# Feed-forward up-projections with the tokens' high and low parts in one 512-column matmul, on one Trainium2 core

## The chip, the cores and the metric

The kernel runs on one core of one Trainium2 chip. The metric is the device time of one launch in microseconds (us); lower is better. The engines of a core are named as in the profile: PE (matrix multiply), PEld (its weight loads), DVE (vector), ACT (scalar), POOL (GpSimd) and SP (which issues the DMAs here).

## What is computed

Two small decoder blocks are run one after the other over the same 256 tokens of width 1024, batch 1, all in float32. The first block has two layers (a gated linear attention layer and a sparse attention layer, each with attention over a memory), and each layer ends in a convolutional feed-forward. The second block has one layer, with a plain gated feed-forward. These three feed-forwards, with an inner width of 2816, are what the change touches:

```python
def conv_ffn(h, w_up, conv_w, conv_b, w_down):
    T = h.shape[1]
    a, b = jnp.split(h @ w_up, 2, axis=-1)
    a_pad = jnp.pad(a, ((0, 0), (CONV_WIDTH - 1, 0), (0, 0)))
    a = sum(a_pad[:, j:j + T] * conv_w[j] for j in range(CONV_WIDTH)) + conv_b
    return (jax.nn.silu(a) * b) @ w_down
...
    n2 = _rmsnorm(h, norm2_w)
    ffn = (jax.nn.silu(n2 @ w_gate.astype(h.dtype)) * (n2 @ w_up.astype(h.dtype))) @ w_down.astype(h.dtype)
    return h + ffn
```

## The kernel before, in words

**Tiling.** Activations lie transposed: 128 partitions are 128 of the 1024 features, and the columns are the 256 tokens (8 chunks c of 128 features). Every float32 matrix product of the projections is made of three matmuls in the type fp32r, a type with fewer bits than float32. Each operand is split into a high part (rounded to fp32r) and a low part (the rest): weights into `wh` and `wl`, tokens into `xh` and `xl`. `mm3` (lines 359 to 362) adds high weights times high tokens, high weights times low tokens, and low weights times high tokens into the same 256 columns of a PSUM bank. The RMS norm's factor per token (`rs`) is applied after the up-projection.

**Weights.** All weights are cut into 146 units of 128 x 2048 float32 (1 MB), used in one fixed order. SP loads unit i into one of three slots of `raw` as soon as DVE has finished with the unit three places before. ACT makes the high part in two halves of 1024 columns (`cast`, line 1891), and DVE the low part in two halves (`rest`, line 1130). The slots of `wh` and `wl` are a ring of three too, so a cast also waits until PE has used the unit three places before (`used`).

**A feed-forward stage** (`ffn`; called f0, f1 and f2) has 22 blocks f of 128 inner features. Unit `u{f}` holds the 1024 x 256 weights of block f, 128 columns for each of the halves a and b (gate and value). `unit_f` (from line 368) does 8 chunks c by 2 halves j by the 3 matmuls of `mm3`, that is 48 matmuls, into one PSUM bank, a in its columns 0 to 255 and b in 256 to 511. Banks 0 to 3 are used in turn. Unit `d{p}` holds the down-projection's weights for blocks 2p and 2p+1; `down` adds 48 matmuls into banks 4 to 7, which collect over the whole stage. The order on PE is u0, u1, sums of the norm, u2, the spread of the norm's factor, u3, d0, then u4, u5, d1 and so on to u20, u21, d9 and d10.

**Between up and down**, for each block: DVE multiplies both halves by `rs` out of PSUM (`mix_in`, lines 1255 or 1257, and 1258); ACT makes the first tap of the convolution (line 1966), DVE the two others (1266, 1274), ACT the SiLU (1975, or 1972 in f2, which has no convolution), DVE the product with b (1280), ACT its high part `fh` (1981) and DVE its low part `fl` (1285). Each step waits for the one before through a semaphore. In the old order DVE and ACT take the steps for two blocks in turn, with the halves of the casts and rests (six a pair of blocks) ahead of and behind them.

After a stage DVE adds the four collecting banks to the residual (line 1309), two chunks a bank, and ACT and DVE split the new chunks for the next stage.

Of the kernel before, what the change touches and what calls it, by code (L numbers as in the profile page):

```python
# [146 lines left out]
MIX = {"f0": 0, "f1": 1, "f2": 2}  # L147
KORD = [0, 1, 2, 3, 4, 5, 6, 7]
# [11 lines left out]
def program(nc, ctx, w_d, x_d, mem_d, meta_d, small_d, const_d, gmask_d, nsac_d, sel_d, out_d):  # L160
# [19 lines left out]
    xh_, xl_ = sb("xh", 8 * TM, F32R), sb("xl", 8 * TM, F32R)  # L180
# [13 lines left out]
    xh, xl = v3(xh_[:, :], TM), v3(xl_[:, :], TM)  # L194
# [3 lines left out]
    XH, XL = (lambda c: xh[:, c, NM:TM]), (lambda c: xl[:, c, NM:TM])  # L198
    XFH, XFL = (lambda c: xh[:, c, :]), (lambda c: xl[:, c, :])
# [19 lines left out]
    def area(n):  # L219
# [13 lines left out]
    YB, AB = arena[:, ARW - 1540:ARW - 516], arena[:, ARW - 516:ARW]  # L233
# [67 lines left out]
    banks = [ctx.enter_context(nc.psum_tensor(f"ps{i}", [128, 512], F32)) for i in range(8)]  # L301
# [26 lines left out]
    f_pad, f_a, f_y, f_z, f_g, f_h, f_l, f_used, f_act = (  # L328
        count("ffn_" + n) for n in ("pad", "a", "tap0", "conv", "b", "hi", "lo", "used", "silu"))
# [25 lines left out]
    def pe_program(pe, t):  # L355
# [12 lines left out]
        def unit_f(name, bank, a_h, a_l, ready, order=KORD):  # L368
# [13 lines left out]
            used[i] = ps.ready(name)  # L382

# [118 lines left out]
        def down(tag, p):  # L502
# [19 lines left out]
            for j in range(2):  # L522
                t.wait_ge(*f_l.at(22 * m + 20 + j))
            t.wait_ge(*w_lo.at(2 * i + 1))
            for o in range(8):
                acc = banks[4 + o // 2][:, (o % 2) * 256:(o % 2) * 256 + 256]
                cs = slice(o * 128, (o + 1) * 128)
                for j in range(2):
                    f = 20 + j
                    last = mm3(acc, H[:, j, cs], L[:, j, cs], fch(fh_, f), fch(fl_, f), False, j == 1)  # L530
                if o % 2 == 1:
                    last.then_inc(*ps.full(f"{tag}acc{4 + o // 2}"))
            used[i] = ps.ready(f"{tag}acc7")

        def ffn(tag):
            x_in = entered(tag)
            unit_f(f"{tag}u0", bank_a(), XH, XL, x_in)
            unit_f(f"{tag}u1", bank_a(), XH, XL, x_in)
            sums(tag, bank_b())
            unit_f(f"{tag}u2", bank_a(), XH, XL, x_in)  # L540
            norm_spread(tag, bank_b(), rst_)
            unit_f(f"{tag}u3", bank_a(), XH, XL, x_in)
            down(tag, 0)
            for p in range(1, 10):
                unit_f(f"{tag}u{2 * p + 2}", bank_a(), XH, XL, x_in)
                unit_f(f"{tag}u{2 * p + 3}", bank_a(), XH, XL, x_in)
                down(tag, p)
            down(tag, 10)
# [572 lines left out]
    def dve_program(v, d):  # L1121
        def rest(*names):

            for name in names:
                i = U[name]
                src, H, L = wslot(raw, i), wslot(wh, i), wslot(wl, i)
                for a in range(2):
                    s = slice(a * HW, (a + 1) * HW)
                    d.wait_ge(*w_hi.at(2 * i + a))
                    v.tensor_tensor(L[:, s], src[:, s], f32(H[:, s]), ALU.subtract).then_inc(*w_lo.up(2 * i + a))  # L1130
                to[0] = i + 1
# [107 lines left out]
        def ffn(tag, cw, tail):  # L1239
            m, k0 = MIX[tag], 22 * MIX[tag]  # L1240
            yb = [YB[:, 0:512], YB[:, 512:1024]]
            ab = [AB[:, 0:T + 2], AB[:, T + 2:2 * (T + 2)]]
            rs = rs_[:, 0:T]
            if cw is not None:
                for n in range(2):
                    last = v.memset(ab[n][:, 0:2], 0.0)
                last.then_inc(*f_pad.up(m))

            def mix_in(f):
                y, b, a, P = yb[f % 2][:, 0:T], yb[f % 2][:, T:2 * T], ab[f % 2], ps[f"{tag}u{f}"]  # L1250
                d.wait_ge(*ps.ready(f"{tag}u{f}"))
                if f >= 2:
                    d.wait_ge(*f_l.at(k0 + f - 2))
                if cw is not None:
                    v.tensor_tensor(a[:, 2:2 + T], P[:, 0:T], rs, ALU.mult).then_inc(*f_a.up(k0 + f))  # L1255
                else:
                    v.tensor_tensor(y, P[:, 0:T], rs, ALU.mult).then_inc(*f_a.up(k0 + f))
                v.tensor_tensor(b, P[:, T:2 * T], rs, ALU.mult).then_inc(*ps.freed(f"{tag}u{f}"))

            def conv(f):  # L1260
                if cw is None:
                    return
                y, a = yb[f % 2][:, 0:T], ab[f % 2]
# [4 lines left out]
            def conv2(f):  # L1268
                if cw is None:
                    return  # L1270
                y, a = yb[f % 2][:, 0:T], ab[f % 2]
# [4 lines left out]
            def gated(f):  # L1276
                y, b = yb[f % 2][:, 0:T], yb[f % 2][:, T:2 * T]
                d.wait_ge(*f_act.at(k0 + f))
                d.wait_ge(*ps.done(f"{tag}u{f}"))
                v.tensor_tensor(b, y, b, ALU.mult).then_inc(*f_b.up(k0 + f))  # L1280
# [6 lines left out]
            square_sums(tag)  # L1287
            rests(f"{tag}u0", 2)
            rests(f"{tag}u1", 2)
            token_variance(tag)  # L1290
            rests(f"{tag}u2", 2)
            take("spread_" + tag, rs, T)
            d.wait_ge(*ps.done("spread_" + tag))
            for p in range(11):
                if p:
                    rests(f"{tag}u{2 * p}", 2)
                    rests(f"{tag}u{2 * p + 1}", 2)
                for step in (mix_in, conv, conv2, gated, low):
                    step(2 * p)
                    step(2 * p + 1)  # L1300
                if p:
                    rests(f"{tag}d{p - 1}", 2)
            rests(f"{tag}d10", 2)
# [11 lines left out]
            tail(3, f"{tag}acc7")  # L1315

# [563 lines left out]
    def act_program(s, a):  # L1880
        def cast(*names):

            for name in names:
                i = U[name]
                src, H = wslot(raw, i), wslot(wh, i)
                for n in range(2):
                    cs = slice(n * HW, (n + 1) * HW)
# [626 lines left out]
```

## Time and profile before

| | |
|---|---|
| time before, median of 3 runs | 975.68 us |
| lowest and highest of them | 974.63 and 980.84 us |
| the profiled execution's own time | 980.05 us |
| its span in the profile | 978.7 us |
| its mean granted PE clock | 0.991 of full speed |
| busy: PE, PEld, DVE, ACT | 952.6, 927.4, 666.1, 501.7 us |
| instructions on PE | 7939 matmuls, each with a weight load |
| read from memory | 158 MB, 163 GB/s over the span |

"Busy" is the time in which at least one instruction of an engine was under way. Matmuls are pipelined, and a matmul's own duration (0.28 us for 256 columns) covers several that follow it: what a stream of matmuls costs is read from the distance between two starts. A granted clock of 1.00 is 2.4 GHz and 0.5 is 1.2 GHz; a stretch with both shows a number between.

### The profile page before, as it was taken

What the parts mean: (1) busy time and instruction counts of PE and PEld (TensorE: products, weight loads), DVE (VectorE), ACT (ScalarE), POOL (GpSimd) and SP (SyncE); (2) the same over time, 40 slices, a digit from 0 to 9 for tenths busy, and PEclk for the clock granted to TensorE, in tenths of its full rate; (3) what the DMA queues carried; (4) which work ended last, traced back from release to release, by engine and by line L of the source; (5) the groups of instructions that cost most, each with busy time, mean ns of one, the idle gap of its engine ahead of it and who ended that gap; (6) DMA issues with size and microseconds to landing.
All of it is one profiled execution on the core that took longest, in us unless ns stands there. A gap on an engine that the chain in (4) does not pass through costs nothing.

```text
span 978.7 us, 18777 instructions
## 1 busy us (share of the span) xinstructions
PE 952.6 (97%) x7939; PEld 927.4 (95%) x7939; DVE 666.1 (68%) x1205; ACT 501.7 (51%) x835; POOL 26.2 (3%) x29
## 2 busy tenths in 40 slices
PE   5998999999999999999999999999999899999998
PEld 5898989999999998889999999999988899999998
DVE  5678866787676779884877767675567377556554
ACT  5554445465454556674664545455235455444441
POOL 0000000000000000000000000000122000000000
PEclk9999999999999999999999999999989999999999
DMA  8443431644535454423446454544231164555541
GB/s 347 168 169 113 147 130 44 259 172 171 210 147 215 170 216 140 173 90 127 143 172 268 176 213 146 212 171 172 87 130 44 47 255 173 178 196 176 186 170 44
DMA packets 24851, 160.66 MB, mean 164 GB/s; under 512 B 2880, under 2 KB 4672, under 8 KB 6080
## 3 DMA queue, kind: packets, MB, share of 16 engines
q1 hardware_dynamic: 24768, 159.46, 44.3%
q8 instruction: 63, 1.03, 0.4%
q14 instruction: 20, 0.16, 0.0%
HBM read 158.14 MB, written 1.05 MB: 163 GB/s over the span
## 4 chain that ended last, share of the span: by engine, by line
PE 88%; DVE 8%; ACT 2%; issue 1%; DMA 1%; SPq 0%; DVEq 0%
PE ps L357 87%; DVE wl L1130 2%; PE ps L366 1%; DMA raw<-in_w 1%; DVE col L1139 1%; ACT wh L1891 0%; DVE arena L1385 0%; DVE arena L1373 0%; ACT arena L2026 0%; ACT arena L2024 0%; DVE arena L1364 0%; DVE arena L1540 0%; DVE arena L1606 0%; SPq L2319 0%; DVE arena L1556 0%
## 5 line engine op out<-in xcount | busy, mean ns | idle before, releaser
L1130 DVE TENSOR_TENSOR wl<-raw,wh 128x1024 fp32r<-128x1024 f32 x292 | 342.0, 1221 | 131.4 <-ACT wh L1891 131.4
L357 PE MATMUL ps<-xh,wh 128*128 128x256 f32 (+1 forms) x1312 | 374.0, 285 | 10.5 <-DVE wl L1130 9.1
L357 PE MATMUL ps<-xl,wh 128*128 128x256 f32 (+1 forms) x1312 | 369.6, 282 | 0.0
L357 PE MATMUL ps<-xh,wl 128*128 128x256 f32 (+1 forms) x1312 | 369.0, 281 | 0.0
L1891 ACT CAST wh<-raw 128x1024 fp32r<-128x1024 f32 x292 | 290.7, 1048 | 144.4 <-PE ps L357 135.9
L357 PEld LDWEIGHTS ps<-xh,wh 128*128 128x128 f32 x1312 | 249.3, 190 | 12.8 <-DVE wl L1130 9.1
L357 PEld LDWEIGHTS ps<-xh,wl 128*128 128x128 f32 x1312 | 249.6, 190 | 0.0
L357 PEld LDWEIGHTS ps<-xl,wh 128*128 128x128 f32 x1312 | 249.3, 190 | 0.0
L357 PE MATMUL ps<-fh,wh 128*128 128x256 f32 x528 | 148.6, 282 | 0.0
L357 PE MATMUL ps<-fl,wh 128*128 128x256 f32 x528 | 148.6, 281 | 0.0
L357 PE MATMUL ps<-fh,wl 128*128 128x256 f32 x528 | 148.3, 281 | 0.0
L357 PEld LDWEIGHTS ps<-fh,wh 128*128 128x128 f32 x528 | 99.3, 188 | 0.1
L357 PEld LDWEIGHTS ps<-fh,wl 128*128 128x128 f32 x528 | 99.4, 188 | 0.0
L357 PEld LDWEIGHTS ps<-fl,wh 128*128 128x128 f32 x528 | 99.3, 188 | 0.0
L357 PE MATMUL ps<-coh,wh 128*128 128x256 f32 x288 | 84.2, 292 | 1.0 <-DVE col L1486 1.0
L357 PE MATMUL ps<-col,wh 128*128 128x256 f32 x288 | 82.5, 286 | 0.0
L357 PE MATMUL ps<-coh,wl 128*128 128x256 f32 x288 | 82.4, 286 | 0.0
L1966 ACT ACTIVATE arena<-arena,small 128x256 f32<-128x256 f32 x44 | 22.5, 511 | 78.5 <-DVE arena L1255 78.2
L357 PEld LDWEIGHTS ps<-coh,wh 128*128 128x128 f32 x288 | 56.4, 196 | 2.0 <-DVE col L1486 1.2
L357 PEld LDWEIGHTS ps<-col,wh 128*128 128x128 f32 x288 | 56.3, 196 | 0.1
L357 PEld LDWEIGHTS ps<-coh,wl 128*128 128x128 f32 x288 | 56.3, 195 | 0.0
L357 PE MATMUL ps<-arena 64*128 64x128 f32 (+11 forms) x472 | 50.3, 315 | 4.4 <-DVE arena L1373 2.4
(214 smaller groups left out, 1044.6 us busy)
## 6 DMA issues: line engine op xcount, KB each, us to landing
raw<-in_w SPq DMA_DIRECT2D x145, 1024.0 KB, 4.8
raw<-in_w SPq DMA_DIRECT2D x2, 512.0 KB, 6.3
arena<-in_mem SPq DMA_DIRECT2D x1, 1024.0 KB, 12.9
out<-xt SPq DMA_DIRECT2D x8, 128.0 KB, 2.0
small<-in_small SPq DMA_DIRECT2D x1, 943.5 KB, 9.4
arena<-in_sel SPq DMA_DIRECT2D x3, 256.0 KB, 6.4
xt<-in_x SPq DMA_DIRECT2D x2, 256.0 KB, 4.3
xt<-in_x SPq DMA_DIRECT2D x1, 512.0 KB, 6.8
```

The source lines that it names most:

```text
L357: return pe.matmul(out, lhsT, rhs, start=start, stop=stop, skip_group_check=True)
L366: return pe.transpose(out, src, cn("ident")[0:m, 0:m])
L1130: v.tensor_tensor(L[:, s], src[:, s], f32(H[:, s]), ALU.subtract).then_inc(*w_lo.up(2 * i + a))
L1139: v.scalar_tensor_tensor(L, src, gain, f32(H), ALU.mult, ALU.subtract).then_inc(*x_lo.up(n))
L1891: s.copy(H[:, cs], src[:, cs]).then_inc(*w_hi.up(2 * i + n))
L1966: s.activation(yb[f % 2][:, 0:T], ab[f % 2][:, 0:T], ACT.Copy, scale=sm(cw, f, f + 1)).then_inc(*f_y.up(k0 + f))
```

## The change

The high and low parts of the tokens become one tensor `xhl`, so that the 256 high and the 256 low columns of a chunk can be one moving operand of two runs. The new `unit_up` takes the place of `unit_f` in the three feed-forwards alone. For each chunk and half it issues two matmuls in place of three: high weights times both token parts, 512 columns, into a whole bank; and low weights times the high part, 256 columns, into the first 256 columns. Half a of a block has one bank and half b the next, so a block fills a pair of banks, and banks 0 to 3 are two pairs used in turn. The two 256-column parts of a bank are added on the way out: ACT copies the second parts of both banks (`second`, 128 x 512), DVE adds the first parts to them (`both`, 128 x 512), and DVE multiplies by `rs` in SBUF (`scale`, 128 x 512). These two take the place of `mix_in`.

The order of the feed-forward on DVE and ACT is new: from the third block on, the steps of one block stand before those of the next, and the halves of casts and rests are set between them, for units one pair ahead. The last down-projection (d10) takes block 20 for the first two banks before it asks for block 21. At the end of a stage one unit's rest is moved behind the addition of the residual.

```diff
+        def unit_up(tag, f, ready):
+            name, pair = f"{tag}u{f}", (f + FIRST[tag]) % 2
...
+            P = [ps.open(f"{name}.{j}", 2 * pair + j) for j in range(2)]
+            for j in range(2):
+                t.wait_ge(*ps.vacant(f"{name}.{j}"))
+            for c in range(8):
+                t.wait_ge(*w_lo.at(2 * i + c // 4))
+                t.wait_ge(*ready(c))
+                for j in range(2):
+                    o = slice(j * 128, (j + 1) * 128)
+                    mm(P[j][:, :], H[:, c, o], XHL(c), c == 0, False)
+                    last = mm(P[j][:, 0:T], L[:, c, o], XH(c), False, c == 7)
+                    if c == 7:
+                        last.then_inc(*ps.full(f"{name}.{j}"))
+            used[i] = ps.ready(f"{name}.1")
...
-            for j in range(2):
+            for j, q in ((0, 0), (0, 1), (1, 0), (0, 2), (1, 1), (0, 3), (1, 2), (1, 3)):
                 t.wait_ge(*f_l.at(22 * m + 20 + j))
...
+            def both(f):
+                P, low = pairs[(f + FIRST[tag]) % 2].rearrange("p (j s t) -> p j s t", j=2, s=2), v3(yb[f % 2], T)
+                d.wait_ge(*f_s.at(k0 + f))
                 if f >= 2:
+                    v.tensor_tensor(two(f), P[:, :, 0, :], low, ALU.add).then_inc(*ps.freed(f"{tag}u{f}.0"))
+                    return
+                for j in range(2):
+                    v.tensor_tensor(two(f)[:, j, :], P[:, j, 0, :], low[:, j, :], ALU.add).then_inc(*ps.freed(f"{tag}u{f}.{j}"))
+
+            def scale(f):
+                d.wait_ge(*ps.done(f"{tag}u{f}.{1 if f < 2 else 0}"))
+                scaled = f_ab.up(2 * m + f) if f < 2 else ps.freed(f"{tag}u{f}.1")
+                v.tensor_tensor(two(f), two(f), bc2(rs), ALU.mult).then_inc(*scaled)
...
+            for p in range(1, 11):
+                x, z, i = 2 * p, 2 * p + 1, U[f"{tag}u{2 * p}"]
+                both(x)
+                scale(x)
+                rest_part(i + 3, 0)
+                conv(x)
+                conv2(x)
+                rest_part(i + 3, 1)
+                gated(x)
+                both(z)
+                low(x)
+                scale(z)
+                if p < 10:
+                    rest_part(i + 4, 0)
+                conv(z)
+                conv2(z)
+                if p < 10:
+                    rest_part(i + 4, 1)
+                gated(z)
+                if p < 10:
+                    rest_part(i + 5, 0)
+                low(z)
+                if p < 10:
+                    rest_part(i + 5, 1)
...
+            def second(f):
+                P = pairs[(f + FIRST[tag]) % 2].rearrange("p (j s t) -> p j s t", j=2, s=2)
+                for j in range(2):
+                    a.wait_ge(*ps.ready(f"{tag}u{f}.{j}"))
+                if f >= 2:
+                    a.wait_ge(*f_l.at(k0 + f - 2))
+                s.copy(v3(yb[f % 2], T), P[:, :, 1, :]).then_inc(*f_s.up(k0 + f))
...
+            for p in range(1, 11):
+                x, z, i = 2 * p, 2 * p + 1, U[f"{tag}u{2 * p}"]
+                second(x)
+                cast_part(i + 3, 0)
+                tap0(x)
+                cast_part(i + 3, 1)
+                silu(x)
+                high(x)
+                second(z)
+                cast_part(i + 4, 0)
+                tap0(z)
+                cast_part(i + 4, 1)
+                silu(z)
+                if p < 10:
+                    cast_part(i + 5, 0)
+                high(z)
+                if p < 10:
+                    cast_part(i + 5, 1)
```

## Rows read from the trace of the kernel before

**Rows 1.** The page, parts 1 and 4: busy time and the chain that ended last.

```profile
PE 952.6 (97%) x7939; PEld 927.4 (95%) x7939; DVE 666.1 (68%) x1205; ACT 501.7 (51%) x835; POOL 26.2 (3%) x29
...
PE 88%; DVE 8%; ACT 2%; issue 1%; DMA 1%; SPq 0%; DVEq 0%
```

**Rows 2.** Windows: the three feed-forward stages, then one up and one down stretch.

```profile
core 0: us, PE busy (x) PEld busy (x) DVE busy (x) ACT busy (x) POOL busy (x), PEclk, DMA share, GB/s
176.33:364.00 187.67, 187.67 (x1597) 187.56 (x1595) 135.09 (x219) 98.78 (x142) 0.70 (x1) 1.00 0.51 188
477.07:664.93 187.86, 187.86 (x1597) 187.63 (x1595) 136.70 (x222) 100.00 (x143) 0.70 (x1) 1.00 0.52 194
788.13:975.91 187.78, 187.74 (x1596) 187.53 (x1594) 113.96 (x173) 82.35 (x114) 1.62 (x1) 1.00 0.48 172
205.63:216.90 11.27, 11.27 (x99) 11.27 (x97) 9.29 (x13) 7.73 (x11) 0.00 (x0) 1.00 0.58 224
216.90:222.59 5.69, 5.69 (x51) 5.69 (x49) 4.71 (x11) 3.94 (x7) 0.00 (x0) 1.00 0.66 240
```

**Rows 3.** Timeline of PE: where that up stretch and that down stretch begin.

```profile
205.63 0.28 PE L357 MATMUL ps<-xh,wh 128*128 128x256 f32 x1
...
216.90 0.28 PE L357 MATMUL ps<-fh,wh 128*128 128x256 f32 x1
```

**Rows 4.** Timeline of PE: four plain fp32 matmuls and what follows.

```profile
117.30 1.02 PE L357 MATMUL ps<-memkv,arena 128*128 128x256 f32 x4
118.16 0.27 PE L366 MATMUL ps<-cst,arena 128*128 128x128 f32 x1
```

**Rows 5.** Timeline of PE: 16 two-column matmuls, then a unit of 48, 272 columns.

```profile
681.18 1.84 PE L357 MATMUL ps<-gw,arena 128*128 128x2 f32 x16
682.88 0.37 PE L357 MATMUL ps<-xh,wh 128*128 128x272 f32 x1
683.09 0.28 PE L357 MATMUL ps<-xl,wh 128*128 128x272 f32 x1
...
688.89 0.29 PE L357 MATMUL ps<-xh,wl 128*128 128x272 f32 x1
```

**Rows 6.** Timeline of PE: first and last of 24 matmuls with narrow weights, twice.

```profile
19.48 0.28 PE L357 MATMUL ps<-xh,smh 128*16 128x256 f32 x1
22.15 0.28 PE L357 MATMUL ps<-xh,sml 128*16 128x256 f32 x1
...
692.78 0.29 PE L357 MATMUL ps<-xh,smh 128*8 128x272 f32 x1
695.64 0.29 PE L357 MATMUL ps<-xh,sml 128*8 128x272 f32 x1
```

**Rows 7.** Window and timeline of PE: 256 columns at a lower granted clock.

```profile
711.00:714.00 3.00, 3.00 (x18) 3.00 (x17) 1.32 (x2) 2.99 (x5) 2.92 (x1) 0.57 0.00 0
...
711.45 0.41 PE L357 MATMUL ps<-wh,xl 128*128 128x256 f32 x1
712.52 0.41 PE L357 MATMUL ps<-wh,xh 128*128 128x256 f32 x1
```

**Rows 8.** Groups by shape on DVE and ACT: feed-forward steps, 128x512 forms.

```profile
L1130 DVE TENSOR_TENSOR wl<-raw,wh 128x1024 fp32r<-128x1024 f32 x58 | 67.5, 1221 | 29.8 <-ACT wh L1891 29.8
L1285 DVE TENSOR_TENSOR fl<-arena,fh 128x256 fp32r<-128x256 f32 x20 | 8.3, 426 | 0.7
L1255 DVE TENSOR_TENSOR arena<-ps,rs 128x256 f32<-128x256 f32 x18 | 7.6, 421 | 13.0 <-PE ps L357 13.0
...
L1167 DVE TENSOR_TENSOR arena<-ps,rs 128x512 f32<-128x512 f32 x7 | 4.7, 686 | 4.5 <-PE ps L357 4.5
L2130 ACT COPY arena<-ps 128x512 f32<-128x512 f32 x4 | 2.3, 587 | 0.0
...
L1891 ACT CAST wh<-raw 128x1024 fp32r<-128x1024 f32 x58 | 57.9, 1048 | 30.3 <-PE ps L357 29.7
```

**Rows 9.** Timeline of DVE: the first low parts of the second feed-forward stage.

```profile
500.12 0.83 DVE L1285 TENSOR_TENSOR fl<-arena,fh 128x256 fp32r<-128x256 f32 x2
```

More of the change, by code:

```diff
@@ L299, in program @@
     r2 = area(16)
-    banks = [ctx.enter_context(nc.psum_tensor(f"ps{i}", [128, 512], F32)) for i in range(8)]
+    pairs = [ctx.enter_context(nc.psum_tensor(f"ps{i}", [128, 1024], F32)) for i in range(4)]
+    banks = [pairs[i // 2][:, i % 2 * 512:(i % 2 + 1) * 512] for i in range(8)]
     ps = Psum(banks, [sem(f"bank_full{i}") for i in range(8)], [sem(f"bank_free{i}") for i in range(8)])
@@ L521, in down @@
                 return
-            for j in range(2):
+            for j, q in ((0, 0), (0, 1), (1, 0), (0, 2), (1, 1), (0, 3), (1, 2), (1, 3)):
                 t.wait_ge(*f_l.at(22 * m + 20 + j))
[L524 to L532, printed above, removed]
+                t.wait_ge(*w_lo.at(2 * i + j))
+                for o in (2 * q, 2 * q + 1):
+                    acc = banks[4 + q][:, (o % 2) * 256:(o % 2) * 256 + 256]
+                    cs = slice(o * 128, (o + 1) * 128)
+                    last = mm3(acc, H[:, j, cs], L[:, j, cs], fch(fh_, 20 + j), fch(fl_, 20 + j), False, j == 1)
+                if j == 1:
+                    last.then_inc(*ps.full(f"{tag}acc{4 + q}"))
             used[i] = ps.ready(f"{tag}acc7")
@@ L1124, in rest, with rest_part @@
             for name in names:
[L1125 to L1131, printed above, removed]
+                for n in range(2):
+                    rest_part(U[name], n)
+        def rest_part(i, n):
+            if i >= len(NAMES):
+                return
+            s = slice(n * HW, (n + 1) * HW)
+            d.wait_ge(*w_hi.at(2 * i + n))
+            v.tensor_tensor(wslot(wl, i)[:, s], wslot(raw, i)[:, s], f32(wslot(wh, i)[:, s]),
+                            ALU.subtract).then_inc(*w_lo.up(2 * i + n))
+            to[0] = i + n
         to = [0]
@@ L1287, in ffn @@
             square_sums(tag)
+            both(0)
             rests(f"{tag}u0", 2)
@@ L1290, in ffn @@
             token_variance(tag)
+            both(1)
             rests(f"{tag}u2", 2)
@@ L1293, in ffn @@
             d.wait_ge(*ps.done("spread_" + tag))
[L1294 to L1303, printed above, removed]
+            for step in (scale, conv, conv2, gated, low):
+                step(0)
+                step(1)
+            for p in range(1, 11):
[22 more added lines that the diff above has]
+                    rest_part(i + 5, 1)
+            rests(f"{tag}d10", 1)
             for q in range(4):
@@ L1315, in ffn @@
             tail(3, f"{tag}acc7")
+            rests(f"{tag}d10", 2)
         gmix0 = lambda c: sm("gmix0", c, c + 1)
@@ L1981, in high @@
                 s.copy(fch(fh_, f), yb[f % 2][:, T:2 * T]).then_inc(*f_h.up(k0 + f))
+            second(0)
             casts(f"{tag}u0", 2)
             casts(f"{tag}u1", 2)
+            second(1)
             casts(f"{tag}u2", 2)
-            for p in range(11):
-                if p:
-                    casts(f"{tag}u{2 * p}", 2)
-                    casts(f"{tag}u{2 * p + 1}", 2)
-                for step in (tap0, silu, high):
-                    step(2 * p)
-                    step(2 * p + 1)
-                if p:
-                    casts(f"{tag}d{p - 1}", 2)
+            for step in (tap0, silu, high):
+                step(0)
+                step(1)
+            for p in range(1, 11):
[16 more added lines that the diff above has]
+                    cast_part(i + 5, 1)
             casts(f"{tag}d10", 2)
```

82 lines of the change are left out of this document (40 added, 42 removed).

## The prediction, made before the changed kernel had run

> **What bounds the kernel now.** I read the page's busy shares and chain first. PE is busy for 97% of the span and PE makes 88% of the chain that ended last [rows 1], so time is won or lost on PE, or where something makes PE wait. Next, the windows over the three feed-forward stages: 187.67, 187.86 and 187.78 us, PE busy in all but 0.04 us, clock 1.00 [rows 2]. Together they are 563 of 978.7 us. DVE is busy for 136.7 of 187.86 us in the fullest (73%), ACT for 100.0 (53%). Inside a stage everything repeats by pairs of blocks: 96 up matmuls in 11.27 us, then 48 down matmuls in 5.69 us [rows 2], from the first up matmul at 205.63 to the first down at 216.90 [rows 3]. So an up matmul of 256 columns costs 11.27/96 = 117.4 ns, and a triple (`mm3`) 352 ns. At 2.4 GHz 256 columns are 106.7 ns, so 10.7 ns of each is something else. This something is all that the change can save: it streams the same 768 columns a triple.
>
> **What 512 columns cost.** The trace has no fp32r matmul of 512 columns. The nearest rows:
> - Plain fp32, 256 columns: four from 117.30 to 118.16, 215 ns each, twice 106.7 and 1.7 more [rows 4]. A full weight load hides behind that almost wholly.
> - Weights of 128 columns with 2 columns streamed: 16 in 1.70 us, 106 ns each [rows 5]. A load takes about as long as 256 columns.
> - Weights of only 16 columns, 256 streamed: (22.15 - 19.48)/23 = 116.1 ns [rows 6]. So 9.4 of the 10.7 ns stay though the load is short: they belong to the matmul.
> - 272 columns: (695.64 - 692.78)/23 = 124.3 ns with 8-column weights [rows 6], (688.89 - 683.09)/46 = 126.1 ns with full ones [rows 5]. Sixteen more columns should be 6.7 ns and are 8.2 and 8.7. This speaks against a cost that is only per instruction.
> - At a granted clock of 0.57, mostly 1.2 GHz, 256 columns take 1.07/5 = 214 ns, 256 at 1.2 GHz and nothing more [rows 7].
>
> Ends for a 512-column matmul: from 215 ns (rows 4, all extra cost hidden) to 117.4 + 256 x (8.7/16 = 0.54) = 257 ns (the steep slope between 256 and 272 columns). Between them lies 234.8 ns, where two matmuls are merged for nothing. I take the extra cost as one per instruction, of the size that the short loads leave, 9.4 ns: the removed matmul saves 9.4, the 512 columns take 225.4, and a triple 342.6 ns. The nearest row for it is the 256-column one with narrow weights; the 272-column rows keep the other side open. The moving operand has two runs; no row shows such a matmul. If its second run begins like a new matmul, the saving is gone, 0 to 9.4 ns, and that is in the second case below.
>
> There are 66 blocks x 8 chunks x 2 halves = 1056 triples: 1056 x 9.4 = 9.9 us off PE. With all 10.7 ns it is 11.3.
>
> The Trainium skill (TensorE: Matmul & The Clock Gate, Part 2, "Back-to-back issue gap") gives an isolated warm matmul N/2.4 + 2.5 ns. The fp32 rows are near it (215 against 213.3 + 2.5), the fp32r rows are not (117.4 against 109.2). By that rule alone the removed matmul would save 2.5 ns and the change 2.6 us: the rule speaks against the change, and by it the time would be some 973.6, within the second case below.
>
> **What it adds on DVE and ACT.** For each block DVE loses two multiplies out of PSUM of 128x256 (421 ns, L1255 and its twin) and gains a 128x512 add out of PSUM and a 128x512 multiply (686 ns each, from L1167) [rows 8]: +0.53 us. ACT gains a 128x512 copy out of PSUM, 587 ns (L2130). A stage adds 22 x 0.53 = 11.7 us to DVE and 12.9 to ACT: 148 and 113 us of some 184.5, 80% and 61%. Both have room. The arithmetic of the shares is not enough, since the steps form a chain, so I laid out one pair, with t = 0 at the end of block x on PE; the loop closes when PE ends the next such block 16.65 us later (16.95 less 32 x 9.4 ns). `second` ends at 0.65, `both` 1.35, `scale` 2.05 (x's banks are free); two rests of 1.22 us [rows 8] and two taps of about 0.48 bring DVE to 5.4, `gated` 5.9; ACT's `high` 6.3 and only then `second(z)` 6.95, for which DVE idles about a microsecond; `both(z)` 7.6, `low(x)` 8.1, `scale(z)` 8.8, then again two rests and taps to 12.2, `gated(z)` 12.6, and rest, low, rest to 15.5. Against PE's needs: x's pair of banks is asked for again at 11.1 and is free at 2.1; the next unit's low weights stand at 3.3 and 5.4, needed at 11.1; low parts 8.1 and 14.3, needed at 22. So PE does not wait; the least slack is the loop itself, 15.5 of 16.65 us. SP's loads hang on the rests: the one behind x's pair is issued at 5.4, and the cast that needs it comes at 17.2; the window of that up stretch moved 224 GB/s [rows 2], 1 MB in 4.7 us. All these additions cost nothing while the loop stays under 16.65 us.
>
> **Entries and ends of stages.** At an entry ACT's copy of block 0 must wait for PE, and ahead of it stand the norm's squares, behind it four casts for u2 and u3. The casts begin there at most 0.6 us later than now, with about 2 us in hand. u2 now needs block 0's banks, which `both(0)` frees before any rest. The first down-projection is tight already: in f1 block 0's low part stands at 500.12 + 0.42 = 500.54 [rows 9] and PE asks at 500.80. PE will come 0.6 us sooner and the chain 0.45 us sooner (it starts at the norm's spread, after three of the four blocks), with taps that start 0.2 later behind a longer `scale`: a wait of 0 to 0.3 us a stage. At the end, f2's third collecting bank is complete 0.7 in place of 1.4 us before the fourth, and its two adds (0.75 us) may delay the last by up to 0.1. The wait of d10 for block 21 is hidden by d9 now and stays so: that block's low part needs about 7 us from its unit's end, d9 and the first quarter of d10 give it 5.69 + 1.42 = 7.1. I take +0.5 us for all of this, between 0 and +1.
>
> **Sum.** -9.9 + 0.5 = -9.4 us on the profiled execution, 980.05 to 970.65. It is 4.4 us above the median of the runs, 975.68, and I carry that difference over unchanged: **966.3 us**. Own range, with 10.7 ns at one end and 6 ns (part of the cost going with the columns) at the other: 964 to 970.
>
> **The rivals.**
> - *The extra cost goes with the columns* (or with each run of the operand). Then 512 columns take twice 117.4. From that go at most 3 ns (the 1.7 of rows 4 and the 117.4 - 116.1 = 1.3 of the absent load), or 3 ns come on top, if the steeper 272-column rows are partly right. The time changes by -3.2 to +3.2 us and the 0.5: 976.2, from 973 to 979.4. For it: 116.1 to 124.3 is a ratio of 1.071 for 1.0625 as many columns, and the clean 214 ns at the low clock, as if a source of operands could not keep up with 2.4 GHz. Against it: even a pure proportion gives 1.0 ns too little there, so addresses matter as well.
> - *The long matmul hides everything*, as the fp32 rows do: 215 + 117.4 = 332.4 ns, -19.7 ns a triple, -20.8 us, with the 0.5 it is 955.4 us. For it: a weight load of 106 ns lies idle behind 213. Against it: narrow weights kept 9.4 of 10.7 ns. Half of that gain would be 965.8.
> - *The other side: the stream gets slower with its length.* Its place is the 512-column matmul alone; it decides from 234.8 ns on. At the slope of 0.54 ns a column it is 257, the triple 374, +22.3 ns, +24.0 us with the 0.5: 999.7 us. At 245 ns: 987. For it: both 272-column rows. Against it: drawn back to no columns the slope gives a negative cost, so it can't be the whole law.
> - *DVE's loop becomes the bound.* It has 1.1 us to spare. From 17.0 us a pair on, the stage is slower than before; at 17.5 us, 30 pairs x 0.55 + 0.5 = +17 us, 993. It would take six handshakes of 0.3 us more than I counted.
>
> **How the numbers follow.** Chances: forecast 0.52, columns 0.24, all hidden 0.12, slower stream 0.07, DVE's loop 0.05. The measurement tells about 1% from no change: 965.9 and 985.4. Half of the forecast's own range lies below 965.9, 0.26, and with "all hidden" faster is 0.38; slower is 0.12; same is the rest, 0.50. The range of 8 in 10 reaches over the first three cases, 954 to 980.
>
> **What would show it.** In the changed profile: up stretches of 64 matmuls for 96, 10.96 us where 11.27 stood (11.15 to 11.35 for the columns' case, 10.6 for all hidden); the start of a 512-column matmul to the next 225 ns; down stretches unchanged at 5.69; stages of 184.5 to 185 us; PE still without waits in them; 1056 matmuls fewer, 6883. DVE near 148 us a stage, ACT near 113. I am wrong if PE's stretches shrink and gaps before `unit_up` or `down` appear (DVE's loop), or if no stretch shrinks.

## The result, and the profile after

The changed kernel takes 981.55 us (median, 978.84 to 984.73); the kernel before, beside it on the same chip, 976.9. The ratio is 1.0041, 95% interval 1.0027 to 1.0054: slower by 0.4%, and within the 1% that counts as no change. The forecast was 966.3, and its range ended at 980. The profiled execution has a span of 983.4 us; it is the slowest of the twenty runs (984.73).

The page's busy shares and the chain by engine, which answer to [rows 1]:

```profile
PE 955.4 (97%) x6883; PEld 885.2 (90%) x6883; DVE 701.6 (71%) x1211; ACT 532.9 (54%) x901; POOL 25.3 (3%) x29
...
PE 88%; DVE 8%; ACT 2%; issue 1%; DMA 1%; SPq 0%; DVEq 0%; ACTq 0%
```

1056 matmuls are gone and PE is busy for 2.8 us more; a part of that can be the clock, a mean of 0.986 here and 0.991 in the profile before. Windows over the three feed-forward stages, then one up and one down stretch, which answer to [rows 2]:

```profile
core 0: us, PE busy (x) PEld busy (x) DVE busy (x) ACT busy (x) POOL busy (x), PEclk, DMA share, GB/s
177.85:365.42 187.57, 187.57 (x1245) 172.40 (x1244) 145.55 (x221) 110.54 (x167) 0.70 (x1) 1.00 0.54 186
480.17:668.12 187.95, 187.78 (x1244) 172.41 (x1243) 147.00 (x224) 111.18 (x166) 0.70 (x1) 1.00 0.54 191
792.53:980.11 187.58, 187.58 (x1244) 172.45 (x1242) 125.21 (x174) 91.84 (x136) 0.71 (x1) 1.00 0.49 171
224.08:235.27 11.19, 11.19 (x66) 9.81 (x65) 9.82 (x15) 6.77 (x10) 0.00 (x0) 1.00 0.57 199
235.27:241.03 5.76, 5.76 (x50) 5.76 (x49) 4.77 (x8) 3.81 (x6) 0.00 (x0) 1.00 0.52 182
```

The stages last what they lasted (187.67, 187.86, 187.78). An up stretch shrank by 0.08 us, 2.5 ns a triple, and the down stretch behind it grew by 0.07, though nothing in it was changed. A pair of blocks takes 16.95 us, as before. The timeline of PE at the start of that up stretch:

```profile
224.08 0.39 PE L362 MATMUL ps<-xhl,wh 128*128 128x512 f32 x1
224.31 0.28 PE L362 MATMUL ps<-xhl,wl 128*128 128x256 f32 x1
224.43 0.39 PE L362 MATMUL ps<-xhl,wh 128*128 128x512 f32 x1
224.66 0.28 PE L362 MATMUL ps<-xhl,wl 128*128 128x256 f32 x1
```

A long one is followed after 0.23 us, a short one after 0.11 to 0.12. Over the whole stretch a triple is 11.19/32 = 349.7 ns; 342.6 was forecast. On DVE and ACT the new passes cost what was worked out. The groups by shape that answer to [rows 8] (the 60 of L1285 are the adds out of PSUM):

```profile
L1157 DVE TENSOR_TENSOR wl<-raw,wh 128x1024 fp32r<-128x1024 f32 x292 | 348.8, 1219 | 45.2 <-ACT wh L1949 45.0
L1949 ACT CAST wh<-raw 128x1024 fp32r<-128x1024 f32 x292 | 296.9, 1046 | 64.0 <-PE ps L362 57.3 <-DMA raw<-in_w 6.8
L1293 DVE TENSOR_TENSOR arena<-arena,rs 128x512 f32<-128x512 f32 x66 | 45.2, 688 | 1.1
L1285 DVE TENSOR_TENSOR arena<-ps,arena 128x512 f32<-128x512 f32 x60 | 41.5, 691 | 92.8 <-ACT arena L2024 92.8
L2024 ACT COPY arena<-ps 128x512 f32<-128x512 f32 x66 | 38.5, 584 | 86.6 <-PE ps L362 86.2 <-DVE fl L1319 0.3
```

### The profile page after: what moved, and what is told of

It is laid out like the page before. It is cut to its first block, busy times and chain, and to the rows that moved or that the text cites. A ratio compares the mean times of both kernels' runs of the same rounds, so it can differ in the third digit from the quotient of the medians.

```text
span 983.4 us, 16578 instructions
## 1 busy us (share of the span) xinstructions
PE 955.4 (97%) x6883; PEld 885.2 (90%) x6883; DVE 701.6 (71%) x1211; ACT 532.9 (54%) x901; POOL 25.3 (3%) x29
## 4 chain that ended last, share of the span: by engine, by line
PE 88%; DVE 8%; ACT 2%; issue 1%; DMA 1%; SPq 0%; DVEq 0%; ACTq 0%
PE ps L362 86%; DVE wl L1157 3%; PE ps L371 1%; DMA raw<-in_w 1%; DVE col L1167 1%; ACT wh L1949 1%; SPq L2398 0%; DVE arena L1440 0%; DVE xhl L1167 0%; DVE arena L1428 0%; DVE xt L1363 0%; ACT arena L2105 0%; ACT arena L2103 0%; DVE arena L1419 0%; DVE arena L1661 0%
## 5 line engine op out<-in xcount | busy, mean ns | idle before, releaser
L362 PE MATMUL ps<-xhl,wh 128*128 128x512 f32 (+2 forms) x1568 | 469.4, 360 | 9.9 <-DVE wl L1157 9.4
L1157 DVE TENSOR_TENSOR wl<-raw,wh 128x1024 fp32r<-128x1024 f32 x292 | 348.8, 1219 | 45.2 <-ACT wh L1949 45.0
L362 PE MATMUL ps<-xhl,wl 128*128 128x256 f32 (+1 forms) x1312 | 370.7, 283 | 0.0
L1949 ACT CAST wh<-raw 128x1024 fp32r<-128x1024 f32 x292 | 296.9, 1046 | 64.0 <-PE ps L362 57.3
L362 PEld LDWEIGHTS ps<-xhl,wh 128*128 128x128 f32 x1568 | 279.5, 190 | 55.9 <-DVE wl L1157 9.4
L362 PEld LDWEIGHTS ps<-xhl,wl 128*128 128x128 f32 x1312 | 248.3, 189 | 0.0
L1285 DVE TENSOR_TENSOR arena<-ps,arena 128x512 f32<-128x512 f32 x60 | 41.5, 691 | 92.8 <-ACT arena L2024 92.8
L2024 ACT COPY arena<-ps 128x512 f32<-128x512 f32 x66 | 38.5, 584 | 86.6 <-PE ps L362 86.2
L362 PEld LDWEIGHTS ps<-arena 64*128 64x128 f32 (+4 forms) x472 | 40.0, 178 | 13.4 <-issue 6.0
```

Source lines behind the costliest of these rows:

```text
L362: return pe.matmul(out, lhsT, rhs, start=start, stop=stop, skip_group_check=True)
L1157: v.tensor_tensor(wslot(wl, i)[:, s], wslot(raw, i)[:, s], f32(wslot(wh, i)[:, s]), ALU.subtract).then_inc(*w_lo.up(2 * i + n))
L1285: v.tensor_tensor(two(f), P[:, :, 0, :], low, ALU.add).then_inc(*ps.freed(f"{tag}u{f}.0"))
L1949: s.copy(wslot(wh, i)[:, cs], wslot(raw, i)[:, cs]).then_inc(*w_hi.up(2 * i + n))
L2024: s.copy(v3(yb[f % 2], T), P[:, :, 1, :]).then_inc(*f_s.up(k0 + f))
```

## Experiments

Two questions: why the merge gave nothing, and where the 0.3 to 0.4% came from. Ratios are to the kernel before on the same chip.

**1. Streams by themselves, and the merge taken back.** The first kernel is nothing but streams of fp32r matmuls; it leaves out all of the reference's work. 

> A kernel of matmul streams alone (it computes nothing of the reference): fp32r, full and 16-column weights, 128 to 512 columns, one run or two, then 256 columns with the start of the moving or the stationary operand shifted by 64 bytes at a time. Theory A (the extra cost goes with the columns, about 9 to 12 percent of them): starts 117 to 120 ns apart at 256 columns, 175 to 180 at 384, 233 to 240 at 512, the same for two runs. Theory B (a cost per matmul, about 10 ns): 224 at 512. Theory C (the weight load is what costs): 16-column weights bring 256 columns to 109 and 512 to 216. If addresses matter, the shifted streams spread between 112 and 121 ns; if they don't, all are equal.

Windows over three of its streams: 24 matmuls of 256 columns, 24 of 512, and 24 pairs of a 512 and a 256. Each also holds the short matmul that marks its end, some 0.11 us. DVE does nothing in this kernel and has no column.

```profile
36.66:39.65 2.99, 2.99 (x28) 2.99 (x27) 0.00 (x0) 0.00 (x0) 1.00 0.00 0
52.56:58.15 5.59, 5.59 (x28) 4.61 (x26) 0.00 (x0) 0.00 (x0) 1.00 0.00 0
72.06:80.65 8.59, 8.59 (x51) 7.46 (x50) 0.00 (x0) 0.00 (x0) 1.00 0.01 2
```

That is 119.7, 228.4 and 353.4 ns by the starts. At this place of the operands 512 columns save 11 ns against twice 256 when they are alone, and 5.7 in turns with short ones. Two runs cost nothing (227.6). The widths between, 24 matmuls each of 320, 384 and 448 columns, and then 16-column weights with 256 and with 512 columns:

```profile
39.65:43.28 3.63, 3.63 (x28) 3.63 (x27) 0.00 (x0) 0.00 (x0) 1.00 0.00 0
43.28:47.58 4.30, 4.30 (x27) 4.30 (x27) 0.00 (x0) 0.00 (x0) 1.00 0.00 0
47.58:52.56 4.98, 4.98 (x28) 4.62 (x26) 0.00 (x0) 0.00 (x0) 1.00 0.02 3
63.73:66.49 2.76, 2.76 (x28) 2.31 (x26) 0.00 (x0) 0.00 (x0) 1.00 0.00 0
66.49:72.06 5.57, 5.57 (x28) 2.39 (x27) 0.00 (x0) 0.00 (x0) 1.00 0.00 0
```

From 256 to 512 columns the cost beyond the columns at 2.4 GHz is 13 to 16 ns. So at this place it is nearly one per instruction, as the forecast had it. Narrow weights take 113.4 ns by the starts for 256 columns, 6.3 less than full ones, but 231.4 for 512, 3 more: the load has a part in the cost at 256 columns. And where only the place of the operands moved, in steps of 64 bytes, 256 columns took 114.1 to 120.0, with a period of 256 bytes. Twice 114.1 is as much as the 512 columns took at the first place. So the cost that I had taken as one per instruction depends on addresses.

Then the changed kernel with the long matmul split again, beside the changed kernel once more.

```diff
-                    mm(P[j][:, :], H[:, c, o], XHL(c), c == 0, False)
+                    mm(P[j][:, 0:T], H[:, c, o], XH(c), c == 0, False)
+                    mm(P[j][:, T:2 * T], H[:, c, o], XL(c), False, False)
```

> The changed kernel with its 512-column matmul cut back into two of 256 columns, into the same bank; banks, adds and order stay as changed. If the merge saves what the changed profile shows in the up stretches (0.07 us a pair, 30 pairs), this is 2 us slower than the changed kernel and some 6 us slower than the kernel before. If the merge itself is to blame for the slower down stretches (5.76 against 5.69), those return to 5.69 and the time is that of the changed kernel or less, 979 to 982. If the loss lies in the order and the added passes, it stays above the kernel before by 3 us or more.

> The changed kernel once more, for a comparison on the same chip: ratio 1.003 to 1.005. If the difference came from where the low granted clock fell in the profiled runs, the new profile has other stretches of it and the feed-forward stages still take 187.6 to 188 us.

Split (k1): 980.09 us, ratio 1.0027 (1.0011 to 1.0043). Merged (a1): 980.46, 1.0027 (1.0012 to 1.0041). Windows of the split kernel, an up and a down stretch:

```profile
221.21:232.47 11.26, 11.26 (x98) 11.26 (x97) 9.88 (x15) 6.80 (x10) 0.00 (x0) 1.00 0.54 195
232.47:238.16 5.69, 5.69 (x50) 5.69 (x49) 4.70 (x8) 3.80 (x6) 0.00 (x0) 1.00 0.51 184
```

Without the merge up is 0.07 longer and down 0.07 shorter: the down stretch's loss is the merge's, and the merge as a whole is worth nothing. The whole 0.27% is in what k1 keeps, the new order and the passes. No run has the one without the other.

**2. The order at the end of a stage.** Taken back in the changed kernel (e1), and made alone in the kernel before (b1):

```diff
-            rests(f"{tag}d10", 1)
+            rests(f"{tag}d10", 2)
...
             tail(3, f"{tag}acc7")
-            rests(f"{tag}d10", 2)
```

> The changed kernel with one edit taken back: at the end of a feed-forward stage DVE's low weights of the second unit ahead are made before the residual is added, as in the kernel before. Theory one, the 2.5 us that all kernels with the new order lose against the one before come from this move (it delays the first units of the stage after, and the granted clock falls once more in that stage): then the time is that of the kernel before, ratio 1.000, up to 1.001. Theory two, the loss is elsewhere (in the feed-forward entries and the 0.07 us of each down stretch): ratio 1.0025 as before.

> The kernel before with that one edit alone: the low weights of the second unit ahead are made behind the addition of the residual. Theory one: ratio 1.0025, the whole loss, and a stretch of low granted clock near 388 us. Theory two: ratio 1.000.

b1: 978.79, 1.0007 (0.9995 to 1.0020). e1: 982.33, 1.0046 (1.0030 to 1.0061). Theory one falls: the moved rest costs nothing in the kernel before, and taking it back makes the changed kernel worse. Then the last down-projection in its old order (e2):

```diff
-            for j, q in ((0, 0), (0, 1), (1, 0), (0, 2), (1, 1), (0, 3), (1, 2), (1, 3)):
+            for j in range(2):
                 t.wait_ge(*f_l.at(22 * m + 20 + j))
...
+            for o in range(8):
+                for j in range(2):
```

> The changed kernel with the last down-projection of a stage in the old order (a bank is completed every 1.42 us, block 21 asked for at once). In the changed kernel PE ends the first stage 0.7 us earlier against DVE's chain of adding banks and PE's idle time near 386 us is 2.1 us in place of 1.5, with a stretch of low granted clock behind it. Theory one, the order of the last down-projection makes this: idle 1.5 us again, no low clock there, the last residual adds 0.3 us closer to PE's end in the third stage, ratio to before 1.000 to 1.001. Theory two, DVE is late because its own chain of steps ends later (its rest of 2.35 us begins 0.4 us later, at 357.76): the bank adds stay where they are, and PE waits a further 0.3 us for block 21; ratio 1.003.

e2: 980.6, 1.0039 (1.0025 to 1.0054). The traces say where each pays. From the starts of the down matmuls I took six times, in us; the time at the low granted clock within it, in us, is in brackets:

| kernel | first stage, first to last down | to the first down of the second | second stage | to the third | third stage | to the end |
|---|---|---|---|---|---|---|
| before | 163.85 | 137.01 | 163.93 | 147.02 (10.2) | 163.85 | 3.15 |
| b1 | 163.85 | 136.83 | 163.89 | 144.93 (6.8) | 163.85 | 3.17 |
| a1 | 163.92 | 138.81 (3.4) | 163.96 | 145.06 (6.8) | 163.92 | 3.56 |
| k1 | 163.85 | 138.90 (3.4) | 163.90 | 145.12 (6.8) | 163.85 | 3.43 |
| e1 | 163.92 | 138.29 | 163.94 | 146.39 (6.8) | 163.92 | 3.53 |
| e2 | 164.58 | 136.95 | 164.64 | 145.17 (6.8) | 163.92 | 3.18 |

(Up to the first down, 199 to 201 us, the runs differ by where the clock falls; nothing is read from that.) The timeline of DVE shows what the changed ones have in common, the low part of the last block of the first stage, in b1 and in a1:

```profile
356.01 0.83 DVE L1285 TENSOR_TENSOR fl<-arena,fh 128x256 fp32r<-128x256 f32 x2
```

```profile
357.42 0.42 DVE L1319 TENSOR_TENSOR fl<-arena,fh 128x256 fp32r<-128x256 f32 x1 [0.47 <-ACT fh L2046]
357.76 2.35 DVE L1157 TENSOR_TENSOR wl<-raw,wh 128x1024 fp32r<-128x1024 f32 x2
360.03 0.75 DVE L1363 TENSOR_TENSOR xt<-ps,xt 128x256 f32<-128x256 f32 x2
```

Block 21's unit ended at 352.39 in b1 and at 351.57 in a1. Its low part is done 4.5 us later in b1 and 6.3 us later in a1, where copy, add and multiply come for one block after the other. In e1 and e2 PE itself waits for this; the waits of PE between 349 and 368 us, e1 first:

```profile
PE ps L362 <- DVE col L1167: 1.0, 1, 1.0
```

```profile
PE ps L362 <- DVE fl L1321: 0.4, 1, 0.4
```

e1 waits at the next stage's entry (the residual stands behind two more rests), e2 for block 21. The changed kernel has neither wait, and pays further on. PE ended the first stage 0.7 us earlier in a1 (363.09 against 363.78), yet DVE adds the last banks at 364.05 in both, and PE then waits for DVE near 387 us; b1, then a1:

```profile
PE ps L366 <- DVE arena L1611: 1.5, 1, 1.5
```

```profile
PE ps L371 <- DVE arena L1665: 2.1, 1, 2.1
```

Behind that wait the granted clock is low for 3.4 us. The windows from 388 to 392, of b1 and of a1:

```profile
388.00:392.00 4.00, 4.00 (x34) 3.97 (x35) 3.93 (x22) 3.97 (x14) 0.00 (x0) 1.00 0.72 270
```

```profile
388.00:392.00 4.00, 4.00 (x22) 3.97 (x22) 3.93 (x21) 3.97 (x14) 0.00 (x0) 0.57 0.68 283
```

The 48 matmuls there take 7.44 us in place of 5.94. The five profiles with a wait of 2.1 us (the changed kernel, a1, k1, g2, g8) have this low clock, and the ten with 1.5 us (before, b1, e1, e2, v0 twice, v1, w1, w2, y1) have not; but a2 and w3 below waited 2.2 and 2.3 and have not either. That the longer wait brings the low clock is thus likely, not shown. a1 against b1 by the table: 1.98 between the first two stages, 0.39 at the end, 0.13 before the third, 0.07 in each stage, 2.7 us in all; the medians of a1 and of the kernel before lie 2.2 apart. e1 against b1, on one chip, is 3.5 us both by the table and by the medians. For e2 the table gives only 1.9 us more than b1, and its median lies 3.8 above the kernel before: half of that is not explained.

The low clock also decides how the runs without a profile fall. On the chip of a1 the kernel before had a mean granted clock of 0.995 in 12 of its 23 runs (median 976.8) and 0.991 in 11 (979.5). a1 had 0.991 in six of twelve (979.5), less in the others (980.2 to 983.7), and 0.995 in none. At 0.991 the two take the same time. What the medians show there is thus mainly that the low clock comes oftener in the changed kernel; what makes it come oftener, no run separates.

**3. The place of the operands.** Streams alone again, over all sixteen pairs of offsets. 

> Streams of matmuls by themselves; nothing of the reference is computed. All 16 pairs of (offset of the weights, offset of the moving columns) in steps of 64 bytes within 256, for three patterns: 256 columns alone, the old triple of three 256-column matmuls, the new triple of one 512-column and one 256-column matmul; then the new triple regrouped in runs of 2, 4 and 8 long matmuls followed by as many short ones. If the extra cost belongs to how the two operands lie against each other, the 256-column streams spread from some 114 to 120 ns over the 16 pairs, and the old triple follows with 342 to 360 ns; the new triple then spreads too. If the earlier 114 ns was an accident of one weight address, the spread goes away once addresses vary by chunk (117 to 120 everywhere). If a 512-column matmul loses its advantage (228 ns in a pure stream) because a short one stands before it, runs of 8 give back most of it: 228 + 118 = 346 ns a triple or less, against some 353 for runs of 1; if the short one pays instead, regrouping changes nothing.

Windows over 12 old triples at a fast pair of offsets, 12 at a slow one, and 12 merged triples at the same pair as the first line, again with 0.11 us of a mark each:

```profile
86.88:91.10 4.22, 4.22 (x41) 4.22 (x39) 0.00 (x0) 0.00 (x0) 1.00 0.00 0
82.45:86.88 4.43, 4.43 (x40) 4.43 (x39) 0.00 (x0) 0.00 (x0) 1.00 0.00 0
156.38:160.72 4.34, 4.34 (x28) 3.78 (x27) 0.00 (x0) 0.00 (x0) 1.00 0.02 4
```

Old triples: 341.6 and 360.0 ns, the ends of the sixteen being 340.3 and 360.4. Merged ones: 348.8 to 354.0; at the places of the two old ones shown, 353.4 in place of 341.6 and 350.6 in place of 360.0. So the merge saved where the old triple was slow and cost where it was fast. The merged triples in groups of two long ones and two short, 32 triples at each of two places:

```profile
212.72:223.97 11.25, 11.25 (x68) 9.83 (x67) 0.00 (x0) 0.00 (x0) 1.00 0.01 1
223.97:235.19 11.22, 11.22 (x68) 9.85 (x67) 0.00 (x0) 0.00 (x0) 1.00 0.00 0
```

That is 348 and 347 ns a triple; groups of eight took 349 and 346.5. I had read these streams as 343.4 to 345.1, which is too low, and the 11.0 us in the expectations of g2 and g8 below come from it; 347 to 348 ns make 11.1.

This pointed at an edit of one line. The down-projections' moving tiles go 64 bytes on, in the kernel before (v0) and in the changed one (a2); the small tiles allocated behind them, which no down-projection reads, go along:

```diff
-    fh_, fl_ = sb("fh", 4 * T, F32R), sb("fl", 4 * T, F32R)
+    fh_, fl_ = sb("fh", 4 * T + 16, F32R)[:, 16:], sb("fl", 4 * T, F32R)[:, :]
```

> The kernel before, with the high and low parts of the blocks (the moving operand of the down-projection) placed 64 bytes further on, so that against the weights they lie as in the fast sections of the streams measured alone (113.4 to 113.9 ns a matmul, where the pair of offsets of the kernel before had 120). Theory one, offsets within 256 bytes decide the extra cost inside the kernel too: down stretches of 48 fall from 5.69 to 5.45 us, 33 of them -8 us, ratio 0.992. Theory two, in the kernel other traffic decides it: 5.69 as before, ratio 1.000.

> The changed kernel with the block tiles 64 bytes further on, the edit that took down stretches from 5.69 to 5.45 us in the kernel before (ratio 0.9942). If the 0.07 us that each down stretch lost with the merge (5.76) is the same kind of cost, it goes too: 5.45, and the merge is then worth its 0.07 us a pair: ratio 0.9965. If the stream keeps a state over the switch from up to down, the down stretches may stay slower than 5.45 (5.65, as in the kernel with both realigned): ratio 1.001.

v0: **970.16 us, ratio 0.9942** (0.9920 to 0.9965), and once more 970.19, 0.9923 (0.9902 to 0.9943). a2: 972.12, 0.9927 (0.9908 to 0.9947). Both beat both kernels, and a2 by more than either of its two cases had. v0 takes 160.90 us from the first to the last down of each stage, where the kernel before has 163.85. Windows of an up and a down stretch, v0 (second run), then a2:

```profile
238.58:249.81 11.23, 11.23 (x99) 11.23 (x97) 7.17 (x8) 4.84 (x6) 0.00 (x0) 1.00 0.56 200
249.81:255.26 5.45, 5.45 (x50) 5.45 (x49) 4.47 (x11) 3.70 (x7) 0.00 (x0) 1.00 0.40 168
```

```profile
222.68:233.96 11.28, 11.28 (x67) 9.88 (x65) 10.32 (x15) 7.21 (x10) 0.00 (x0) 1.00 0.61 215
233.96:239.40 5.44, 5.44 (x50) 5.44 (x49) 4.45 (x8) 3.81 (x6) 0.00 (x0) 1.00 0.56 193
```

A down stretch went from 5.69 to 5.45, as the first theory of v0 has it. With the merge the up stretch is even 0.05 longer. Next the up-projections: each chunk of weights 64 bytes beyond its token chunk along the cycle of four, with v0's shift kept (v1), and the matmuls of the changed kernel regrouped (g2, g8).

```diff
+    def skew(buf, i):
+        return v3(buf[:, (i % NH) * SW:(i % NH + 1) * SW], 528)
...
+            return skew(buf, i)[:, c % 4, c // 4 * T + o.start:c // 4 * T + o.stop]
```

```diff
+                    for j in range(2):
+                        mm(P[j][:, :], H[:, c, o(j)], XHL(c), c == 0, False)
...
+                    for j in range(2):
+                        last = mm(P[j][:, 0:T], L[:, c, o(j)], XH(c), False, c == 7)
```

> The kernel before, with the shift of the block tiles and with the chunks of the up-projections' weights laid out so that each chunk stands 64 bytes beyond its token chunk, modulo 256, all along the cycle of four that the token stride of 1088 bytes makes. Matmuls and their order are as in the kernel before. Theory one: up stretches of 96 fall from 11.27 to 10.9 us and down stretches from 5.69 to 5.45; 66 blocks times 48 times 3.9 ns = -12 us and -8 us, together -20 us, ratio 0.98. Theory two: nothing, ratio 1.000. If the casts and low weights suffer from the broken-up layout, DVE and ACT groups get longer than 1.22 and 1.05 us and the gain is smaller.

> The changed kernel with the up-projection's matmuls regrouped: for each chunk the two 512-column ones (halves a and b) one after the other, then the two 256-column ones. Same matmuls, same columns. Measured alone, the new triple took 348.8 to 354 ns where long and short take turns and 343.4 to 344.5 ns in groups of two. Theory one, a 512-column matmul saves its 9 to 11 ns only behind another long one, and loses half of it behind a short one: up stretches of 64 fall from 11.19 to 11.0 us, 33 of them -6 us, ratio to before 0.997. Theory two, in the kernel, whose chunks change their offset, the turn-taking isn't what eats it: 11.19 again, ratio 1.003.

> The same with groups of eight long matmuls (four chunks) followed by eight short ones. Measured alone 344.3 to 345.1 ns a triple. Theory one: 11.0 us, as with groups of two, ratio 0.997; if the turn itself costs, a little less than that, since there are four times fewer turns. Theory two: 11.19.

v1: 977.06, 0.9994 (0.9978 to 1.0010); up 11.34 and down 5.65. g2: 980.83, 1.0021 (1.0007 to 1.0036); g8: 980.79, 1.0023 (1.0008 to 1.0038); up 11.22 and 11.20 to 11.22. The hoped-for gain came in none of the three: the offset relation read from the streams alone does not carry over, and turn-taking isn't what eats the gain. v1 shows one thing more. In its second stage the same matmuls with the same offsets keep another pace from the first up stretch to the last; a window of an up stretch of the first stage, then of the second:

```profile
206.42:217.75 11.33, 11.33 (x98) 11.33 (x97) 9.26 (x13) 7.69 (x11) 0.00 (x0) 1.00 0.60 223
507.44:518.67 11.23, 11.23 (x98) 11.23 (x97) 9.42 (x13) 7.87 (x11) 0.00 (x0) 1.00 0.62 230
```

Last, the third stage's tokens at a constant offset, chunks 1024 bytes apart: w1 at the offset of the shifted block tiles, w2 at a slow one, w3 like w1 with merged matmuls, y1 at a fourth pair.

```diff
+    XG = lambda buf: (lambda c: buf[:, 48 + c * T:48 + (c + 1) * T])
...
+            XU, XUL = (XGH, XGL) if tag == "f2" else (XH, XL)
...
+        at = (i % NH) * SW + (16 if NAMES[i][:3] == "f2u" else 0)
```

(The last line is y1's alone, and moves the weights.)

> The kernel before with the block tiles 64 bytes on, and in the third feed-forward stage alone the token chunks 1024 bytes apart in place of 1088, all of them at the offset against the weights that the shifted block tiles have. Theory one, the offset decides: the up stretches of that stage fall from 11.23 to 10.9 us as the down stretches fell (5.45 for 48), 11 of them -3.6 us against the kernel with the tiles shifted alone, ratio to before 0.990 to 0.991. Theory two, up-projections have a cost of their own: 11.2, ratio 0.994.

> The same with the token chunks of the third stage at the offset that took 119.7 ns a matmul when measured alone. Theory one: its up stretches take 11.5 us, more than the 11.23 of the cycling offsets. Theory two: 11.2.

> The changed kernel with the tiles shifted and the third stage's tokens constant at the offset of the first of these runs. Measured alone the merged triple took 353 ns there against 341.6 for three matmuls. Theory one: up stretches of 64 in the third stage take 11.2 to 11.3 us, no better than with cycling offsets, and 0.3 us worse than three matmuls at the same offset: the merge then costs. Theory two, the merge saves its columns' worth at any offset: 10.9 minus 0.07, 10.8 us.

Windows of an up and a down stretch of the third stage, w1, w2, w3:

```profile
913.11:924.41 11.30, 11.30 (x98) 11.30 (x97) 5.39 (x6) 4.42 (x5) 0.00 (x0) 1.00 0.62 199
924.41:930.07 5.66, 5.66 (x51) 5.66 (x49) 4.55 (x8) 3.07 (x5) 0.00 (x0) 1.00 0.38 162
```

```profile
912.31:923.81 11.50, 11.50 (x99) 11.50 (x97) 5.39 (x6) 4.42 (x5) 0.00 (x0) 1.00 0.57 209
923.81:929.27 5.46, 5.46 (x51) 5.46 (x49) 4.55 (x8) 3.06 (x5) 0.00 (x0) 1.00 0.33 140
```

```profile
913.87:925.17 11.30, 11.30 (x66) 9.81 (x65) 6.70 (x8) 5.52 (x8) 0.00 (x0) 1.00 0.58 190
925.17:930.83 5.66, 5.66 (x51) 5.66 (x49) 4.23 (x6) 2.80 (x4) 0.00 (x0) 1.00 0.48 179
```

w1 and w3 are the answer to the first question. At the same offset, 96 matmuls and 64 take the same 11.30 us: the long one starts the next after 235 ns, twice 117.7. The merge saves nothing at all there. But w1 missed the 10.9 us, and its down stretches went back to 5.66 although their own operands stayed where v0 has them, while behind w2's slow up stretches they keep 5.46. The very first up stretch of w1's third stage, which no down stretch of that stage precedes, did take the 10.9 us (at y1's offsets, below, it took 11.31):

```profile
782.37:793.28 10.91, 10.91 (x99) 10.91 (x98) 9.85 (x17) 6.57 (x11) 0.00 (x0) 1.00 0.57 194
```

So the pace of a stream depends on its offsets and on what ran before it. w1 as a whole: 972.58, 0.9936 (0.9916 to 0.9956). w2 and w3, one run each, are read for their stretches alone.

> The kernel before with the block tiles 64 bytes on; in the third stage the token chunks 1024 bytes apart at their old offset and the up-projections' weights 64 bytes on. Measured alone this pair took 113.4 ns. Theory one, a change of offset on entering lets the stream run fast: up stretches of the third stage 10.9 us, down stretches 5.45, that stage 157.5 us in place of 160.9 from the first down matmul to the last; against the tiles shifted alone -3.6 us. Theory two, the state is kept from the stretch before in some way that the streams measured alone don't show: up 11.3 or 11.5, down 5.65, and no gain.

y1: 971.04, 0.9937 (0.9915 to 0.9960). Its third stage had up 11.31, down 5.46. The down stretch is fast behind an up stretch at another pair of offsets, as theory one has it, but up stays at 117.7 ns, where the stream alone had 113.4. From the first down to the last the stage takes 161.88 us, more than v0's 160.90. The best kernel remains v0.

## Why the prediction was wrong

**The step that failed: "I take the extra cost as one per instruction".** The 10.7 ns beyond 106.7 were read rightly from [rows 2], and the 116.1 ns of narrow weights [rows 6] speak against the weight load as the cause of most of them (alone, at another place, narrow weights took off 6.3 of 13.0). From that it doesn't follow that they belong to the instruction: they could as well belong to the columns, and in this kernel the triples behave so. The long matmul took some 231 ns in place of 225.4, the triple 349.7 in place of 342.6, and at constant offsets 235 + 118, exactly three times 117.7. The term of -9.9 us was 0: -2.5 ns x 1056 = -2.6 us in the up stretches, and +0.07 us in each of the 33 down stretches, +2.3. It is no law of the columns either: streams alone had a cost nearly per instruction at one place of the operands (m1), and merging a triple there took off 9 ns at one place and added 12 at another (m2). What the cost consists of stays open; it was no fixed price of the instruction that could be carried from one stream to another. "Down stretches unchanged at 5.69" failed with it. The first rival, "the extra cost goes with the columns", came nearest, and the rows for it, the 272-column ones [rows 5, 6] at a ratio of 1.071 for 1.0625 as many columns, were in the text. I set them aside because pure proportion left 1.0 ns over; the same rows had shown that "addresses matter as well", and a cost that addresses change by 6 ns can't be told from a fixed one by a difference of 1.

**Plain fp32 as a lower end** [rows 4] was no guide: no fp32r stream came near 215 ns for 512 columns.

**The rule on the back-to-back gap.** By the 2.5 ns of the Trainium skill (TensorE: Matmul & The Clock Gate, "Back-to-back issue gap") the change would have saved 2.6 us. No run here shows it for fp32r: at 256 columns the streams kept 6.7 to 13.3 ns beyond 106.7.

**DVE and ACT: right.** 147.0 and 111.2 us in the fullest stage (148 and 113 forecast), new passes of 0.69, 0.69 and 0.58 us, PE without waits in the loop. **Entries:** 0.2 us in the second stage, as forecast (k1 has it too).

**The ends of stages, mis-sized.** I took +0.5 us, 0 to +1, for entries and ends; the new order and passes cost 2.2 by the medians and some 2.7 by the traces of a1 and b1. The parts were seen: block 21's low part "about 7 us" after its unit (6.3), and the bank adds bunched up. But I priced them as delays on PE at that place. What they delay is DVE's chain into the next stage, and that comes due 24 us later as 0.6 us of waiting, and the stretch of low clock behind it, likely its doing, costs 1.5 us (7.44 less 5.94); and 0.3 to 0.4 at the end of the last stage in place of 0.1. The columns' case with 2.2 us in place of its 0.5 gives 977.9, a ratio of 1.0023 to the 975.68 shown; measured were 1.0041 and 1.0027. Of the 15.3 us between forecast and median, 9.9 are the first term, 1.7 the ends at their size in a1, and 1.2 the kernel before, which took 976.9 this time. The 2.4 left are not traced; half of the twenty runs had a mean clock under 0.99, against 4 of the 12 of a1.

## What to carry to other kernels

Take a stream's distance between starts as a rate of the columns until another width shows otherwise; a fixed cost per instruction needs two widths at the kernel's own addresses and between its own neighbours, not two kinds of weights. Even two widths measured alone misled here: 11 ns saved in the stream, nothing in the kernel. Where the distance is above the ideal, try where the operands lie before changing the matmuls: 64 bytes of padding gave 0.6 to 0.8% here, and removing an eighth of the matmuls nothing. An order that keeps PE free of waits inside a loop can still bill its last turn to the stage behind, so follow the slower engine past the loop's end.

## What was not expected of the hardware

256 fp32r columns at the full clock took 113.4 to 120 ns with the same instructions, set by the place of the weights and of the moving operand within 256 bytes, in steps of 64, and in the whole kernel also by the stream before: the same down stretch took 5.45 us behind an up stretch at 120 or at cycling offsets and 5.66 behind one at its own offset. One up stretch of the whole kernel ran at 113.6 ns (w1, 10.91 us), and those behind it at 117.7. What in the chip makes these paces, and how to keep the up-projections at 113 to 114 ns inside the kernel, stays open.
